# Half-width doubling steps in a triangular inverse, and the last stores of two stages: one change to a two-layer decoder step on one Trainium2 core

## The reference, cut to what matters

```python
q, k, v, iq, ik, iw, gate = _split(xn @ w_in, ATT_SIZES)
y_p = y_p + _gated_out(_att_prompt(q, k, v, iq, iw, ik), gate, att_w_out[l])
...
a_mat = bb[..., :, None] * kk * jnp.where(strict, decay, 0.0)
rhs = bb[..., None] * (vb - jnp.exp(gcum)[..., None] * jnp.einsum('bhcd,bhdv->bhcv', kb, S))
u = lax.linalg.triangular_solve(eye + a_mat, rhs, left_side=True, lower=True, unit_diagonal=True)
```

## Time and profile before

| | us |
|---|---|
| three runs | 2253.71, 2243.04, 2238.78 |
| their median | 2243.04 |
| the profiled execution: its time | 2238.33 |
| the profiled execution: its span, first to last instruction | 2236.5 |
| its mean granted TensorE clock, as a share of full speed | 0.966 |

### The profile page before, as it was taken

The page is one execution under the profiler, slowest core; times in us unless marked ns, Lnnn a source line. Parts: engine busy times, 40 slices in busy tenths (PEclk is TensorE's granted clock), DMA queues, the critical chain, the costliest instruction groups (busy, mean ns, idle before and its releaser), DMA issues. The chain is left out here.

```text
span 2236.5 us, 25198 instructions
## 1 busy us (share of the span) xinstructions
PE 2082.5 (93%) x9079; PEld 1258.4 (56%) x9079; DVE 1408.0 (63%) x2471; ACT 688.1 (31%) x1756; POOL 520.2 (23%) x546
## 2 busy tenths in 40 slices
PE   6999999999989889989899999999989889999998
PEld 5554543444445565655443556666543687777774
DVE  2488987599978878938858422222332576666662
ACT  3445642121223433321101222221111544443441
POOL 2111200000000000001110567777301513322320
PEclk9999999999999999989999999999999899999999
DMA  4024312101123212021211344444638162232210
GB/s 129 15 78 151 114 57 96 36 24 47 47 101 144 85 39 85 19 73 43 76 52 57 106 140 138 138 139 142 215 132 296 57 195 65 66 89 74 74 46 29
DMA packets 157891, 207.33 MB, mean 93 GB/s; under 512 B 43808, under 2 KB 107608, under 8 KB 157720
## 3 DMA queue, kind: packets, MB, share of 16 engines
q1 hardware_dynamic: 134936, 152.87, 21.2%
q0 software_dynamic: 16896, 50.35, 7.4%
q10 hardware_dynamic: 5936, 2.49, 0.4%
HBM read 161.94 MB, written 43.74 MB: 92 GB/s over the span
## 5 line engine op out<-in xcount | busy, mean ns | idle before, releaser
L1737 PE MATMUL acc_ch<-xnT,w_ch 128*128 128x512 f32 x736 | 346.9, 619 | 7.3 <-ACT x_pad L1771 7.3
L1737 PEld LDWEIGHTS acc_ch<-xnT,w_ch 128*128 128x128 f32 x736 | 138.7, 197 | 158.2 <-issue 151.2
L793 PE MATMUL acc<-w_qg,xnT 128*128 128x512 f32 (+1 forms) x432 | 191.9, 598 | 5.4 <-DVE sgate L915 5.4
L1627 POOL DMA_INDIRECT kg<-in_cache_k,rowidx x128 | 132.2, 1033 | 138.6 <-DVE rowidx L1895 79.1
L952 DVE MAX8 top_v<-scores 128x8 f32<-128x4100 f32 x32 | 141.7, 4427 | 0.5
L954 DVE FIND_INDEX8 top_i<-top_v,scores 128x8 uint32<-128x4100 f32 x32 | 141.5, 4423 | 0.0
L956 DVE MATCH_REPLACE8 scores<-top_v,scores 128x4100 f32<-128x4100 f32 x32 | 141.2, 4413 | 0.0
L1634 POOL DMA_INDIRECT home<-in_cache_v,rowidx x128 | 129.3, 1010 | 39.0 <-issue 33.8
L793 PEld LDWEIGHTS acc<-w_qg,xnT 128*128 128x128 f32 (+1 forms) x432 | 78.0, 185 | 103.6 <-issue 97.7
L2697 PE MATMUL PB<-home,ogT_dn 128*128 128x512 f32 x288 | 129.2, 603 | 4.7 <-DVE rhs L2970 3.9
L793 PE MATMUL acc<-w_kvq,xnT 128*128 128x512 f32 (+1 forms) x288 | 127.4, 600 | 3.5 <-PEq L545 3.5
(11 more groups left out here) (423 smaller groups left out, 3924.8 us busy)
## 6 DMA issues: line engine op xcount, KB each, us to landing
home<-in_dn_w_in SPq DMA_DIRECT2D x7, 2048.0 KB, 8.5
w_ch<-in_dn_w_in SPq DMA_DIRECT2D x24, 512.0 KB, 4.9
qkv_d<-y_ch SPq DMA_DIRECT2D x24, 512.0 KB, 6.2
qkv_t<-qkv_d SPq DMA_DIRECT2D x8, 1536.0 KB, 8.0
x<-in_x_all SPq DMA_DIRECT2D x9, 512.0 KB, 3.9
out_y_all<-y_t SPq DMA_DIRECT2D x9, 512.0 KB, 2.7
w_z_s<-in_dn_w_in SPq DMA_DIRECT2D x1, 4160.0 KB, 13.7
w_kvq<-in_att_w_in SPq DMA_DIRECT2D x2, 2048.0 KB, 10.9
```

Of the source, the lines that this page charges most:

```text
L793: ins = pe.matmul(acc[rows(n), k % ACC, :], xnT[:, kk, cols(n)], w[:, kk, :], start=(kk == 0), stop=(kk == KT - 1))
L1627: pool.indirect_dma_start(kg[:, j % KR, :], None, ck, bass.IndirectOffsetOnAxis(ap=rowidx[:, u % 2, t * QT + u // 2:t * QT + u // 2 + 1], ...
L1737: ins = pe.matmul(acc[:, s, :], w[:, c % WR, k, :], xT[:, k, s * 512:(s + 1) * 512], start=(k == 0), stop=(k == KT - 1))
```

## The change

Three edits. In the head stage the last block has a function of its own, `store_last`: it stores v and k as soon as DVE has normed the block, then the gate when formed, then qT when it is out of PSUM. In the attention stage the two waits for y1's stores at the end are gone; `load(n)` of `dn_inputs` waits in their place, for n = 6 and 7. In the scan, levels 4 and 5 work on strips: of blocks of 2^l columns every second one (64 of 128 columns), in the moving operand, in PSUM, in the copy and in the subtraction. At level 5 the change of T is formed for 64 partitions and 32 columns. For the first prompt block (n = 1) Y is still formed and copied at full width. Level 4's Y goes to `kdm[0]`, level 6's to a quarter of L.

```diff
+            def store_last():
+                n, par = m - 1, (m - 1) % 2
+                out = slice(n * P, (n + 1) * P)
+                sp.wait_ge(nat_ok, n + 1)
+                sp.dma_start(d["v_all"][out, :], v_nat[:, n, :]).then_inc(st[par], 16)
+                sp.dma_start(d["k_all"][out, :], raw[:, par, DM:QK]).then_inc(st[par], 16)
+                sp.wait_ge(acc_rd, gate_at[n, 4])
+                sp.dma_start(d["gate_d"][out, :], sgate[:, par, :]).then_inc(st[par], 16)
+                sp.wait_ge(tp_evac, 3 * n + 3)
+                sp.dma_start(d["qT_d"][out, :], qTb[:].rearrange("p a b -> p (a b)")).then_inc(st[par], 16)
...
                 if n == m - 1:
                     first_block()
-                store(n)
+                    store_last()
+                else:
+                    store(n)
...
-            for u in range(2):
-                sp.wait_ge(y_out[u], 16 * (NB // 2))
...
             def load(n):
+                if n >= NB - 2:
+                    sp.wait_ge(env["stores"][f"y1_out{n % 2}"], 16 * (NB // 2))
                 sp.dma_start(x[n % XR], d["y1_d"][rows(n), :]).then_inc(x_in[n % XR], 16)
...
+        def strips(n, l):
+            return n >= 1 and l in (4, 5)
+        def strip(t, l, s):
+            return t.rearrange("p (b s c) -> p b s c", s=2, c=1 << l)[:, :, s, :]
+        def mid(l):
+            return kdm[0] if l == 4 else Y
+        Yq = L[0:64, 1, :, 64:]
...
-                            ins = pe.matmul(a4(("Y", n, l, r))[:, h, :], L[:, lnum(n, l) % 2, hh, :], TT[:, p, hh, :], start=True, stop=True)
+                            dst, src = a4(("Y", n, l, r))[:, h, :], TT[:, p, hh, :]
+                            if strips(n, l) and n >= 2:
+                                dst, src = strip(dst, l, 1), strip(src, l, 1)
+                            ins = pe.matmul(dst, L[:, lnum(n, l) % 2, hh, :], src, start=True, stop=True)
...
-                            ins = pe.matmul(a4(("dTT", n, l, r))[:, h, :], T[:, hh, :], Y[:, hh, :], start=True, stop=True)
+                            dst, src = a4(("dTT", n, l, r))[:, h, :], mid(l)[:, hh, :]
+                            if strips(n, l):
+                                dst, src = strip(dst, l, 1), strip(src, l, 1)
+                            ins = pe.matmul(dst, T[:, hh, :], src, start=True, stop=True)
...
-                            ins = pe.matmul(a4(("dT", n, l, r))[:, h, :], Y[:, hh, :], T[:, hh, :], start=True, stop=True)
+                            dst = a4(("dT", n, l, r))[:, h, :]
+                            if l == 5:
+                                ins = pe.matmul(dst[0:64, 0:32], Y[:, hh, 0:64], T[:, hh, 0:32], start=True, stop=True)
+                            elif l == 4:
+                                ins = pe.matmul(strip(dst, l, 0), mid(l)[:, hh, :], strip(T[:, hh, :], l, 0), start=True, stop=True)
+                            else:
+                                ins = pe.matmul(dst, Y[:, hh, :], T[:, hh, :], start=True, stop=True)
...
-                        dve.tensor_tensor(TT[:, p, hs(r), :], TT[:, p, hs(r), :], a4(("dTT", n, l, r)), ALU.subtract).then_inc(a_dve, 1)
+                        old, new = TT[:, p, hs(r), :], a4(("dTT", n, l, r))
+                        if strips(n, l):
+                            old, new = all_strips(old, l, 1), all_strips(new, l, 1)
+                        dve.tensor_tensor(old, old, new, ALU.subtract).then_inc(a_dve, 1)
...
+                        if l == 5:
+                            old, new = old[0:64, :, 0:32], new[0:64, :, 0:32]
+                        elif l == 4:
+                            old, new = all_strips(old, l, 0), all_strips(new, l, 0)
+                        dve.tensor_tensor(old, old, new, ALU.subtract).then_inc(a_dve, 1)
```

More of the change, by code:

```diff
@@ L2354, in by_blocks, with all_strips @@
             return n >= 1 and l == 6
+        def strips(n, l):
+            return n >= 1 and l in (4, 5)
+        def strip(t, l, s):
+            return t.rearrange("p (b s c) -> p b s c", s=2, c=1 << l)[:, :, s, :]
+        def all_strips(t, l, s):
+            return t.rearrange("p h (b s c) -> p (h b) s c", s=2, c=1 << l)[:, :, s, :]
+        def mid(l):
+            return kdm[0] if l == 4 else Y
+        Yq = L[0:64, 1, :, 64:]
         ua, ub = [], []
@@ L2608, in level @@
                         if by_blocks(n, l):
-                            ins = pe.matmul(a4(("dTT", n, l, r))[0:64, h, 64:], T[0:64, hh, 0:64], Y[0:64, hh, 64:], start=True, stop=True)
+                            ins = pe.matmul(a4(("dTT", n, l, r))[0:64, h, 64:], T[0:64, hh, 0:64], Yq[:, hh, :], start=True, stop=True)
                         else:
-                            ins = pe.matmul(a4(("dTT", n, l, r))[:, h, :], T[:, hh, :], Y[:, hh, :], start=True, stop=True)
+                            dst, src = a4(("dTT", n, l, r))[:, h, :], mid(l)[:, hh, :]
+                            if strips(n, l):
+                                dst, src = strip(dst, l, 1), strip(src, l, 1)
+                            ins = pe.matmul(dst, T[:, hh, :], src, start=True, stop=True)
                     ins.then_inc(fa, 1)
@@ L2754, in level @@
                     if by_blocks(n, l):
-                        act.copy(Y[0:64, hs(r), 64:], a4(("Y", n, l, r))[0:64, :, 64:]).then_inc(a_act, 1)
+                        act.copy(Yq[:, hs(r), :], a4(("Y", n, l, r))[0:64, :, 64:]).then_inc(a_act, 1)
+                    elif strips(n, l) and n >= 2:
+                        act.copy(all_strips(mid(l)[:, hs(r), :], l, 1), all_strips(a4(("Y", n, l, r)), l, 1)).then_inc(a_act, 1)
                     else:
-                        act.copy(Y[:, hs(r), :], a4(("Y", n, l, r))).then_inc(a_act, 1)
+                        act.copy(mid(l)[:, hs(r), :], a4(("Y", n, l, r))).then_inc(a_act, 1)
             def read_state(n):
@@ L2929, in level @@
                     else:
-                        dve.tensor_tensor(TT[:, p, hs(r), :], TT[:, p, hs(r), :], a4(("dTT", n, l, r)), ALU.subtract).then_inc(a_dve, 1)
+                        old, new = TT[:, p, hs(r), :], a4(("dTT", n, l, r))
+                        if strips(n, l):
+                            old, new = all_strips(old, l, 1), all_strips(new, l, 1)
+                        dve.tensor_tensor(old, old, new, ALU.subtract).then_inc(a_dve, 1)
                     if l < last(n):
                         dve.wait_ge(fa, ra.filled(("dT", n, l, r)))
-                        dve.tensor_tensor(T[:, hs(r), :], T[:, hs(r), :], a4(("dT", n, l, r)), ALU.subtract).then_inc(a_dve, 1)
+                        old, new = T[:, hs(r), :], a4(("dT", n, l, r))
+                        if l == 5:
[3 more added lines that the diff above has]
+                        dve.tensor_tensor(old, old, new, ALU.subtract).then_inc(a_dve, 1)
             def base(n):
```

## The result

The changed kernel took 2267.63 us (median of four runs, 2260.92 to 2285.55), the kernel before 2242.6 (four, 2238.78 to 2253.71). The ratio is 1.0125, with an interval of 1.0089 to 1.0161: slower by more than 1%, where half a per cent of gain was forecast. The profiled execution took 2260.92 us, its span 2259.1, and its granted clock was 0.947 in place of 0.966.

A forecast was written before the change was run, and what follows sets the result against it. It took PE, then DVE's products into o_t behind level 5's last subtraction, to bound the scan. Savings of 8.0 + 1.7 + 2.3 = 12.0 us gave a forecast of 2230 us, 8-in-10 range 2216 to 2244.

The forecast's parts named there:

- What bounds the kernel: Scan blocks: PE is busy nearly throughout, but the chain passes to DVE's products into o_t behind level 5's last subtraction.
- Part 1: Scan, levels 4 and 5 on strips: output transposes' second half starts 1.0 us earlier per block, 8.0 us over eight blocks.
- costed at nothing: Scan: the rest of the strips' effects, such as ACT's shorter copy and full-weight matmuls on PE, taken to save nothing.
- Part 2: Head stage's end, stores reordered so qT lands last: next stage starts 1.7 us earlier, bounds 0.8 and 2.1.
- the sharing with the gate: Head's end: gate and qT, 512 KB each, follow closely and share DMA engines; 0.3 us taken off the gain.
- Part 3: Attention's end: removing the wait for y1's stores saves 2.3 us, bounds 1.5 and 2.5.
- PE's time goes with its columns: Rival, scan: strips of 64 columns run at 59 ns, 32 us more saved, 2199 us; chance 5%.
- Strips cost more than whole rows: Rival, scan: gapped PSUM and SBUF access slows strips, 29 us lost at three times their share, 2260 us; chance 5%.
- 53 ns for the stream of a strip: Scan: a strip's assumed share of stream time, hidden under the weights' load unless it exceeds 112 ns.
- the clock falls: Rival, scan: PE's lighter load loses the granted clock; 2244 us, or 2255 if levels are caught; chance 6%.
- 1.6 us a fall: Clock rival's price for a stretch at 1.2 GHz in a block, 13 us if once in every block.

The follow-up runs named there:

- c_narrow5: Changed kernel, but all matmuls of levels 4 and 5 at full width except level 5's narrow change of T; 2227.81 us, ratio 0.9916 to before.
- d_packed: Changed kernel, but the strips' results lie side by side in PSUM without gaps; 2250.55 us, ratio 1.0024 to before.
- a_stores: Kernel before with only the two store edits (head's and attention's ends), scan unchanged; 2237.73 us, ratio 0.9964 to before.
- b_pefull: Changed kernel, but every matmul of levels 4 and 5 at full width; strips only in ACT's copies and DVE's subtractions; 2228.8 us, ratio 0.9936.
- e_strips4: c_narrow5 with all three steps of level 4 on strips on PE; 2254.45 us, ratio 1.0041 to before.
- g_filler: Changed kernel plus one unused 128 x 512 matmul per block between level 4's Y and first change of TT; 2229.64 us, ratio 0.9925.
- h_small_filler: Changed kernel plus four unused matmuls of 4 moving columns at g_filler's place; 2328.18 us on a slower chip, ratio 1.0063 to before.
- k_full_and_filler: c_narrow5 plus g_filler's unused wide matmul; 2292.35 us on a slower chip, ratio 0.9921 to before.

## Why the prediction was wrong, step by step

**"What bounds the kernel": right.** PE and DVE's products meet at the end of level 5, and what shortened them shortened the block.

**Part 1, "1.0 us per block": right at full clock.** Blocks that kept it took 48.08 us (forecast 48.0, was 48.99), 0.9 less. Strips with weights of 128 x 128 stay 112 ns apart, narrow ones 61 ns (forecast 59), each change of shape 0.09 us, DVE's last subtraction 0.28 us (forecast 0.26). One term was costed at nothing and gives a little: moving strips on PE, 0.1 us a block, as c_narrow5's 48.18 shows.

**Part 2: 1.3 us, forecast 1.7.** The mis-sized term is the sharing with the gate. The forecast had 2.6 for the landing, 0.3 for the sharing and 0.5 behind it, 3.4; the way from qT's issue to PE's start measured 3.86, of which 3.4 are the landing, so the sharing cost 0.8. In three experiments this way is shorter than before by 0.5 (a_stores, where qT took 4.2 us to land), 1.1 (b_pefull, 3.6) and 1.4 us (c_narrow5, 3.3), so its size varies from one execution to the next, and once lies below the lower bound of 0.8.

**Part 3: 2.35 us, forecast 2.3.**

**Rival "PE's time goes with its columns": wrong** by the 112 ns. **"Strips cost more than whole rows": this is not what happened**: a half step of eight takes 0.89 us at full clock, and the same in d_packed without gaps in PSUM. The rival's 53 ns for the stream of a strip stands in no row of it. The changed kernel's trace gives nearly the same: its four instructions of 512 columns (L2585) take 1.82 us to the next one's start (2107.11 to 2108.93), which makes an estimate of 57 ns for 64 columns and 114 for 128. So a strip's stream fills about half of the 112 ns, where a full-width one fills them.

The Trainium skill, "PSUM — Partial Sum Buffer", Specifications, says that any non-contiguous pattern slows matmuls significantly. For runs of 16 or 32 elements of fp32 no slowing shows in this kernel's time, 0.89 us with gaps or without; one of the stream by less than a factor of two would be hidden in the 112 ns, so the runs bound the rule here and don't refute it.

**Rival "the clock falls": this is what happened**, and the step that failed is the one that priced and weighed it. It was given 6%, for one reason: "the window shown at 1.00 is one of six on end". But in those six PE streamed levels 4 and 5 at full width. They could say nothing of a kernel that takes half of that stream away, and the first prompt block, at 0.97, had shown that the clock can fall in this scan. The change turned on exactly what that reason took as given. The prediction's own finding in part 1 should have given warning: if strips stay 112 ns apart, PE issues as many instructions in the same time as before, on half the columns, and its busy time doesn't show that. The price was also too small. "1.6 us a fall", and "3 us" were the levels caught, both assume a short stretch. The runs show 20.5 us at 1.2 GHz and 8.4 us a block in its place, in three to five of six blocks: once the clock is down, everything up to `norm_in` runs in it. e_strips4 gives the price near that assumed, 3.3 us, where level 5 is at full width. Four blocks hit make 33.7 us; the six blocks' gain at full clock, 294.4 less 6 x 48.08, is 5.9, and less 0.7 for a short loss 5.2; the difference is the +28.5 of the table.

What told the clock from its rivals: no other theory explains that a matmul more makes the kernel 26.5 us faster (g_filler), that the same time filled with 4 columns doesn't (h_small_filler), and that k_full_and_filler gains nothing from it.

The Trainium skill, "TensorE: Matmul & The Clock Gate", "A second HAM failure mode: psum-queue depth-cycling", tells of small idle times between groups of matmuls by which the clock swings. The pause before the first change of TT is such a one (0.80 us), but it was there before too, at 0.75, with the clock at 1.00, and h_small_filler has falls without it. So by the runs here the pause isn't sufficient, nor is it necessary.

**What stays open.** Four things are left without an answer. One is why seven of twelve blocks of the changed kernel are hit and all those of e_strips4, and another what sets the 21 us. The third is what in the wide matmul keeps the clock, its columns or its values. The last is the short losses, some 21 us behind a mark and of some 0.7 us each, which nearly all versions show in one or two of the six blocks, a_stores with the scan of before among them; the profiled execution of the kernel before has one in its first prompt block (L2554's 3.61 us) and none in the six. No run here tried these by themselves.

## What to carry to other kernels

In this kernel, narrowing the moving operand of fp32 matmuls whose spacing is set by the weights' load saved PE next to no time (0.1 us a block) and cost it its clock; narrow the weights instead, or the work of the engines that read the result (0.4 us a block each). Where a change makes PE's stream thinner, the granted clock of the kernel before, under its fuller stream, is no evidence: price a long stretch at 1.2 GHz through everything that follows on PE, and look at the granted clock by block first when the result is in. If a block is caught, one wide matmul into a free bank, at a place where PE waits anyhow, tells within one run whether it is the clock.

## What was not expected of the hardware

- Useless work made the kernel faster: one 128 x 512 matmul per block, 0.96 us, took it from 2256.14 to 2229.64 us. Four 128 x 4 matmuls of the same 0.97 us at the same place left it at 1.0063 of the kernel before.
- The granted clock fell under uninterrupted PE work: in h_small_filler PE is busy for all of the 20 us ahead of a fall, and in the changed kernel the longest idle time near it is 0.80 us. The fall starts 5 to 7 us behind the mark. It lasts 21 us (once 17) where level 5 is on strips and 7 us (once 10) where it is full width.
- Gaps in PSUM cost no time here: 0.89 us for eight instructions either way.
- A change of the weights' shape costs 0.09 us here. The Trainium skill, "TensorEngine Tiling (Array Packing)", says that a change of the tiling mode drains the engine and gives no figure. The trace shows a cost of this size where the weights go from 128 x 128 to 128 x 64 or 64 x 64; whether a drain is its cause, no run shows.
